# A chunk-wise first stage with columns and shifts on ScalarE, and two combinations of h made from negated halves and accumulating transfers

## Chip, cores and metric

One core of one Trainium2 chip runs the whole program as one launch. The metric is the device time in microseconds, the median of several runs. All arithmetic is fp32; each large product is made in three passes of fp32r matmuls, from a value's high part and its low part (the value less its high part): high x high, high x low, low x high.

## The reference, cut to what matters

A transformer of two layers with three sublayers each (feed-forward, mixer, feed-forward; the mixers are a pooling mixer and a latent attention), and two hybrid attention layers behind it. x is 512 tokens x 1024 features. The change touches the start of the program and the beginning of each of the four feed-forward stages:

```python
sc = jax.nn.silu(c)                                  # c: 1 x 1024
mod = (sc @ ada_w[i] + ada_b[i]).reshape(B, 9, D)    # ada_w[i]: 1024 x 9216
...
h = rmsnorm(x, g_pre) * (1.0 + scale) + shift        # shift, scale: rows 3k, 3k+1 of mod
gate, up = jnp.split(h @ w_in, 2, axis=-1)           # w_in: 1024 x 5632
y = (jax.nn.silu(gate) * up) @ w_out                 # w_out: 2816 x 1024
x = x + weight * (1.0 + gate_row) * rmsnorm(y, g_post)
```

## The kernel before

Everything lies transposed: features on the 128 partitions, tokens along the free dimension. x and h are eight chunks (c = 0 to 7) of 128 features x 512 tokens. Weights arrive in units of 128 x 1024 (512 KB) on SyncE's queue; ScalarE writes a unit's high part (`split_hi`, L444), VectorE its low part (`split_lo`, L459), TensorE multiplies (`three_passes`, L486). Four stages are feed-forward: ffn0, ffn1, ffn2, ffn3; between them lie pool and mla, and behind them two hybrid layers.

**The start.** X is loaded whole on ScalarE's queue; params, `ones` and `ident` on SyncE's. The 16 row blocks of ada_w for shift and scale (8 MB, `ada_first`) come in pairs on SyncE's and GpSimd's queues. VectorE multiplies them by silu(c) and adds them up (`first_rows_dve`, L840 to L860), TensorE closes both sums over partitions with one-column matmuls (`shift_pe` L836, `ada_close_pe` L896). ScalarE squares X chunk by chunk, TensorE sums each chunk's squares (L554), VectorE takes the reciprocal of the root and TensorE spreads it over partitions (`spread_pe`, L571). Only when all of shift and scale is there does `pre_dve`/`pre_act` make h: VectorE scales (L646), ScalarE writes h_hi (L632) and h_full (L635) with the shift as bias, VectorE writes h_lo (L655). TensorE then multiplies units 0 and 1 chunk by chunk and units 2 and 3 one after the other (`ffn_pe`, L1032).

**The beginning of a feed-forward stage.** Units 0 to 3 are plain. The other 20 column blocks of w_in go in ten "pairs" by Winograd's scheme of seven products per 2 x 2 block product (`pair_pe`, products 0 to 6, 24 matmuls of 256 columns each). For this four combinations of h's quarters are made once per stage: U, T2, T3, T4 (`combine_dve`, L1235). VectorE makes all four, each 128 x 1024: U = even chunks' first half of tokens less their second half; T2 = U + odd chunks' second half; T3 = odd second half less even second half; T4 = T2 less odd first half. ScalarE writes their high parts (`combine_hi_act`, L1128), VectorE their low parts over the sums themselves (`combine_lo_dve`, L1253; t_lo and t_sum share memory). Product 0 needs unit 4, product 1 unit 5 and U, product 2 unit 6 and T2, product 3 unit 7, product 4 unit 8 and T3, product 6 unit 10 and T4.

**What sets the order.** Each engine has its own instruction list, written out by hand, which runs in order; waits are on semaphores. GpSimd issues two kinds of transfers in order: the accumulating load that adds one weight unit to another (`add_weights`, L1306) and the loads of the later rows of ada_w (`ada_piece`, L1311), whose products VectorE takes between its other work (`ada_block_dve`, L885), two rows in each pair and the rest in the second half of the stage.

## Time and profile before

| | us |
|---|---|
| median of 3 runs (lowest, highest) | 2941.68 (2940.72, 2943.49) |
| the profiled execution | 2942.72 |
| its span | 2940.9 |
| TensorE busy in the span | 2807.1 (95%) |
| VectorE busy | 2184.5 (74%) |
| ScalarE busy | 1423.5 (48%) |
| GpSimd busy | 402.4 (14%) |

Times in rows are microseconds from the span's start, durations too unless ns stands there. PE is TensorE's matmul side, PEld its weight loads, DVE is VectorE, ACT ScalarE, POOL GpSimd, SP SyncE. One fp32 matmul makes two records. L444 is line 444 of the kernel.

### The profile page before, as it was taken

The page shows a single profiled execution, that of the slowest core. Times are in us where ns is not written, and L with a number is a line of the kernel's source. Part 1 is how long each engine was busy: PE and PEld are TensorE (multiplying, and loading weights), DVE is VectorE, ACT ScalarE, POOL GpSimd, SP SyncE. Part 2 cuts the span into 40 slices and gives each one's busy share as a digit, 9 for nine tenths or more (in the row PEclk, how much of TensorE's full clock was granted, in tenths as well). Part 3 has the DMA queues.
Part 4 walks back from the last instruction along what each step waited for, and adds up shares of the span by engine and source line. Part 5 has one row for each costly group of instructions (what it writes and reads, how often), then busy time and mean ns, then how long its engine had stood idle before and what let it go on. Part 6 is the DMA issues. An engine that isn't in the chain of part 4 may idle for free. (4 is left out here: it accounts for less than half of the span.)

```text
span 2940.9 us, 42829 instructions
## 1 busy us (share of the span) xinstructions
PE 2807.1 (95%) x16742; PEld 2452.6 (83%) x16742; DVE 2184.5 (74%) x3415; ACT 1423.5 (48%) x2356; POOL 402.4 (14%) x299
## 2 busy tenths in 40 slices
PE   7999989999999999889999999999899999999999
PEld 7998878998889988667789988887788778877887
DVE  6888678888788887789687755477777663876773
ACT  4455234455245552466455542463655434555552
POOL 1100102100100101100300000313300233141003
PEclk9999999999999999999999999999999999999999
DMA  6765641765636756200235533302211232022113
GB/s 247 214 207 173 225 154 34 222 210 168 220 123 201 225 161 215 81 18 19 100 101 159 151 101 100 129 22 77 95 51 56 95 122 79 28 95 72 51 58 115
DMA packets 100393, 365.82 MB, mean 124 GB/s; under 512 B 11616, under 2 KB 12384, under 8 KB 99552
## 3 DMA queue, kind: packets, MB, share of 16 engines
q1 hardware_dynamic: 72464, 257.25, 25.1%
q0 software_dynamic: 25280, 92.29, 11.5%
q10 hardware_dynamic: 2448, 13.54, 1.2%
q8 instruction: 134, 2.20, 0.3%
q14 instruction: 67, 0.55, 0.1%
HBM read 354.64 MB, written 6.29 MB: 123 GB/s over the span
## 5 line engine op out<-in xcount | busy, mean ns | idle before, releaser
L444 ACT ACTIVATE w_hi<-raw 128x1024 fp32r<-128x1024 f32 x353 | 368.0, 1052 | 299.1 <-DMA raw<-stream_in 188.2
L465 POOL TENSOR_TENSOR w_lo<-raw,w_hi 128x1024 fp32r<-128x1024 f32 x111 | 278.6, 2516 | 1296.4 <-ACT w_hi L444 1296.4
L486 PE MATMUL psum<-h_hi,w_hi 128*128 128x256 f32 (+1 forms) x1607 | 349.4, 329 | 15.0 <-DVE w_lo L459 9.6
L486 PE MATMUL psum<-h_hi,w_lo 128*128 128x256 f32 (+1 forms) x1607 | 343.1, 325 | 0.0
L486 PE MATMUL psum<-h_lo,w_hi 128*128 128x256 f32 (+1 forms) x1607 | 342.8, 325 | 0.0
L444 ACT ACTIVATE w_hi<-xr 128x1024 fp32r<-128x1024 f32 x200 | 211.3, 1057 | 264.7 <-DVE xr L1169 95.0
L459 DVE TENSOR_TENSOR w_lo<-raw,w_hi 128x1024 fp32r<-128x1024 f32 x202 | 247.2, 1227 | 87.6 <-ACT w_hi L444 87.5
L486 PE MATMUL psum<-t_hi,w_hi 128*128 128x256 f32 (+1 forms) x1536 | 284.5, 300 | 17.3 <-DVE a_lo L1091 8.8
L486 PEld LDWEIGHTS psum<-h_hi,w_hi 128*128 128x128 f32 x1607 | 251.7, 189 | 49.2 <-DVE w_lo L459 12.9
L486 PE MATMUL psum<-t_hi,w_lo 128*128 128x256 f32 (+1 forms) x1536 | 282.7, 299 | 0.0
L486 PEld LDWEIGHTS psum<-h_hi,w_lo 128*128 128x128 f32 x1607 | 252.7, 189 | 26.7
L486 PEld LDWEIGHTS psum<-h_lo,w_hi 128*128 128x128 f32 x1607 | 252.6, 189 | 26.9
L459 DVE TENSOR_TENSOR w_lo<-xr,w_hi 128x1024 fp32r<-128x1024 f32 x160 | 195.7, 1223 | 93.5 <-ACT w_hi L444 93.4
L486 PE MATMUL psum<-t_lo,w_hi 128*128 128x256 f32 (+1 forms) x1472 | 262.1, 294 | 0.0
L486 PEld LDWEIGHTS psum<-t_hi,w_hi 128*128 128x128 f32 x1536 | 220.2, 188 | 33.7 <-issue 11.9
L486 PEld LDWEIGHTS psum<-t_hi,w_lo 128*128 128x128 f32 x1536 | 221.6, 188 | 10.6
L486 PEld LDWEIGHTS psum<-t_lo,w_hi 128*128 128x128 f32 x1472 | 209.1, 188 | 8.0
L885 DVE SCALAR_TENSOR_TENSOR ada_raw<-ada_raw,silu_row 128x1024 f32<-128x1024 f32 x128 | 156.0, 1220 | 46.1 <-DMA ada_raw<-ada_in 45.9
L1311 POOL DMA_DIRECT2D ada_raw<-ada_in x126 | 67.0, 532 | 848.6 <-DVE ada_raw L885 844.4
L486 PE MATMUL psum<-a_lo,w_hi 128*128 128x512 f32 x704 | 177.1, 392 | 0.0
L486 PEld LDWEIGHTS psum<-a_lo,w_hi 128*128 128x128 f32 x704 | 132.6, 188 | 29.2
L1527 ACT ACTIVATE pt_hi<-psum 128x512 fp32r<-128x512 f32 (+3 forms) x160 | 74.6, 466 | 119.6 <-PE psum L1478 117.6
(510 smaller groups left out, 5550.8 us busy)
## 6 DMA issues: line engine op xcount, KB each, us to landing
raw<-stream_in SPq DMA_DIRECT2D x353, 512.0 KB, 3.4
ada_raw<-ada_in POOLq DMA_DIRECT2D x128, 512.0 KB, 5.4
xr<-stream_in SPq DMA_DIRECT2D x120, 512.0 KB, 4.6
xr<-stream_in POOLq DMA_DIRECT2D x40, 512.0 KB, 5.5
ada_first<-ada_in POOLq DMA_DIRECT2D x4, 1024.0 KB, 16.7
ada_first<-ada_in SPq DMA_DIRECT2D x4, 1024.0 KB, 22.1
x_held<-X ACTq DMA_DIRECT2D x2, 2048.0 KB, 6.8
X<-x_held ACTq DMA_DIRECT2D x2, 2048.0 KB, 8.3
```

The costliest lines, as they stand in the source:

```text
L444: act.activation(w_hi[:, u % RING], tile, ACT.Copy, scale=-1.0 if u in negated else 1.0).then_inc(hi_ready, 1)
L459: op = dve.tensor_tensor(w_lo[:, u % RING], source[u][0], low, ALU.subtract)
L465: pool.tensor_tensor(w_lo[:, u % RING], source[u][0], w_hi[:, u % RING].bitcast(F32), ALU.subtract).then_inc(lo_ready, 1)
L486: mm = pe.matmul(dst, w[wi], m[mi], start=(first and n == 0), stop=(last and n == total - 1), skip_group_check=skip)
L885: dve.scalar_tensor_tensor(out=row, in0=row, scalar=1.0, in1=silu_row[:], op0=ALU.mult, op1=ALU.mult, accum_out=mod[:, j, n:n + 1]).then_i ...
L1311: pool.dma_start(ada_raw[:, t % 2], ada[t]).then_inc(ada_loaded[t % 2], 16)
L1527: turned_hi.give(act.activation(A["place"](0, t, rows, n, i), psum[0:rows, 6 + k % 2, 0:n * P].rearrange("p (a n) -> p a n", n=P), ACT.Cop ...
```

## The change

Start: X comes in four pieces on SyncE's queue, with the blocks of ada_w behind it one by one, chunk c's scale block and then its shift block, and weight units 0 to 3 between them (2 and 3 go to the pair buffers); GpSimd loads nothing there. The first eight columns of params and `ident` come on ScalarE's queue. silu(c) is spread over a row by eight matmuls. The squares of X are summed by VectorE, then by TensorE once. scale is a dot product on VectorE for each chunk, shift one too for chunks 2, 4, 6, 7, and a matmul sum for chunks 0, 1, 3, 5. ScalarE makes the two columns of each chunk and then h_hi and h_full from h_full = X * rstd. TensorE multiplies units 0 and 1 with each chunk and units 2 and 3 with chunks that came earlier; filler matmuls (`keep_busy`) are added.

Each feed-forward stage: VectorE makes U and T2 alone. ScalarE writes the negated half of each chunk into T3 or T4 (8 activations of 128 x 256), and GpSimd issues two accumulating transfers, from h_full into T3 and from T2 into T4. In ffn1 and ffn2 two rows of ada_w move from the first pair to the second half of the stage.

```diff
...
+            if L == "ffn0":
+                plan_loads(u, u + 2)
+                for v, slot in ((u + 2, pair_slots[2]), (u + 3, pair_slots[0])):
+                    home[v] = (slot, None, cur.d)
+                    source[v] = (slot.tile, slot.sem, slot.plan())
+                    slot.free = (lo_ready, v + 1)
+                    cur.d += 1
...
+        def first_squares_act(act):
+
+            for c in range(NC):
+                if c % 2 == 0:
+                    act.wait_ge(x_loaded[c // 2], 16)
+                sq_ready.give(act.activation(square_tiles[c], X[:, c], ACT.Square, scale=1.0 / 32), ("ffn0", "pre", c))
+                if c == 3:
+                    act.wait_ge(row_spread, 1)
+                    act.activation(silu_row[:, 0:S], psum[:, 0], ACT.Copy)
+                    act.activation(silu_row[:, S:D], psum[:, 1], ACT.Copy).then_inc(row_ready, 1)
+            full_root_act(act, "ffn0")
...
+        def first_squares_dve(dve, order):
+
...
+            for c in range(1, NC):
+                dve.wait_ge(sq_ready.sem, sq_ready.at(("ffn0", "pre", c)))
+                op = dve.tensor_tensor(total, total, square_tiles[c], ALU.add)
+                if c < NC - 1:
+                    order.step(op)
+                else:
+                    x_squares.give(op, ("ffn0", "pre"))
...
         def full_pe(pe, L):
-            for c in range(NC):
-                pe.wait_ge(sq_ready.sem, sq_ready.at((L, "pre", c)))
-                sums.give(column_sums(pe, sq[:, c % 2], 4, 0, first=(c == 0)), (L, "pre", c))
+            pe.wait_ge(x_squares.sem, x_squares.at((L, "pre")))
+            sums.give(column_sums(pe, square_tiles[0], 4, 0, first=True), (L, "pre", NC - 1))
...
+                    if c:
+                        negate_act(act, L, c - 1)
                 if between is not None:
                     between(c)
+            if L in FFNS:
+                negate_act(act, L, NC - 1)
+
+        def negate_act(act, L, c):
+
+            x, part = ((T3, slice(HALF, S)), (T4, slice(0, HALF)))[c % 2]
+            act.wait_ge(full.sem, full.at((L, c)))
+            act.activation(t_sum[:, x, c // 2], h_full[:, c, part], ACT.Copy, scale=-1.0).then_inc(parts_negated, 1)
...
+        def row_pe(pe):
+
             pe.wait_ge(value.sem, value.at("silu_c"))
...
+                mm = pe.matmul(psum[:, k // 4, k % 4 * P:k % 4 * P + P], silu_c[:, k:k + 1].broadcast_to((P, P)),
+                               ident[:], start=(k % 4 == 0), stop=(k % 4 == 3), skip_group_check=True)
+            mm.then_inc(row_spread, 1)
+
+        def shift_pe(pe, c):
+
+            pe.wait_ge(first_loaded[c][0], 16)
+            for k in range(NC):
+                mm = pe.matmul(psum[:, 6, c:c + 1], first_block(c, 0)[:, k * P:k * P + P], silu_c[:, k:k + 1],
+                               start=(k == 0), stop=(k == NC - 1), skip_group_check=True)
+            mm.then_inc(shift_sums, 1)
...
+        def columns_act(act, c):
+
+            g = col.at["norm_g"] + c
+            act.wait_ge(mod_blocks, c + 1)
+            act.activation(acol[:, c:c + 1], mod[:, 1, c:c + 1], ACT.Identity, scale=par[:, g:g + 1],
+                           bias=par[:, g:g + 1]).then_inc(columns_made, 1)
+            made = c + 1 + sum(e < c for e in SHIFT_BY_PE)
+            if c in SHIFT_BY_PE:
+                b = col.at["ada_b"] + c
+                act.wait_ge(shift_sums, SHIFT_BY_PE.index(c) + 1)
+                act.activation(mod[:, 0, c:c + 1], psum[:, 6, c:c + 1], ACT.Identity,
+                               bias=par[:, b:b + 1]).then_inc(columns_made, 1)
+                made += 1
+            else:
+                act.wait_ge(shift_by_dve, c - sum(e < c for e in SHIFT_BY_PE) + 1)
+            act.wait_ge(columns_made, made)
...
+        def first_chunk_act(act, c):
+
+            act.wait_ge(scaled.sem, scaled.at(("ffn0", c)))
+            part_hi.give(act.activation(h_hi[:, c], h_full[:, c], ACT.Identity, scale=acol[:, c:c + 1],
+                                        bias=mod[:, 0, c:c + 1]), ("ffn0", c))
+            full.give(act.activation(h_full[:, c], h_full[:, c], ACT.Identity, scale=acol[:, c:c + 1],
+                                     bias=mod[:, 0, c:c + 1]), ("ffn0", c))
...
+        def dot_dve(dve, row, j, n):
+
+            b = col.at["ada_b"] + NC * j + n
+            return dve.tensor_tensor_reduce(out=row, in0=row, in1=silu_row[:], op0=ALU.mult, op1=ALU.add, scale=1.0,
+                                            scalar=par[:, b:b + 1], accum_out=mod[:, j, n:n + 1])
+
+        def first_dots_dve(dve, c):
+
+            dve.wait_ge(first_loaded[c][1], 16)
+            dot_dve(dve, first_block(c, 1), 1, c).then_inc(mod_blocks, 1)
+            if c not in SHIFT_BY_PE:
+                dve.wait_ge(first_loaded[c][0], 16)
+                dot_dve(dve, first_block(c, 0), 0, c).then_inc(shift_by_dve, 1)
...
+        def first_chunks_dve(dve, u0):
+
+            dve.wait_ge(spread.sem, spread.at(("ffn0", "pre")))
+            first_scale_dve(dve, 0)
+            split_lo(dve, u0)
+            split_lo(dve, u0 + 1)
+            first_low_dve(dve, 0)
+            for c in range(1, NC):
+                first_scale_dve(dve, c)
+                first_dots_dve(dve, c)
+                if c == 1:
+                    split_lo(dve, u0 + 2)
+                    continue
+                first_low_dve(dve, c - 1)
+                if c == 2:
+                    split_lo(dve, u0 + 3)
+            combine_u_dve(dve, "ffn0")
+            first_low_dve(dve, NC - 1)
...
-        FIRST_ROWS = {"ffn0": 2, "ffn1": 0, "ffn2": 0}
+        ROWS = {"ffn0": (16, 64), "ffn1": (64, 104), "ffn2": (104, 144), "ffn3": (144, 144)}
+        SHIFT_BY_PE = (0, 1, 3, 5)
+        FIRST_ROWS = {"ffn0": 2, "ffn1": 0, "ffn2": 0, "ffn3": 0}
+        PAIR_ROWS = {"ffn0": range(9), "ffn1": range(1, 9), "ffn2": range(1, 9), "ffn3": ()}
...
+        def first_chunks_pe(pe, L, u0, g0):
+
+            late = {2: (0, 1), 3: (2,), 4: (3,), 5: (4,), 6: (5,), 7: (6, 7)}
...
+            for c in range(NC):
+                if c in SHIFT_BY_PE[1:]:
+                    shift_pe(pe, c)
+                pe.wait_ge(h_ready.sem, h_ready.at((L, c)))
+                for m in range(2):
+                    chunk(m, c)
+                for m in range(2, 4):
+                    for late_c in late.get(c, ()):
+                        chunk(m, late_c)
+                if c < 2:
+                    keep_busy(pe, 7, 6)
...
+                row_pe(pe)
+                pe.wait_ge(small_loaded, 32)
+                keep_busy(pe, 7, 12)
                 full_pe(pe, L)
-                shift_pe(pe)
+                keep_busy(pe, 7, 4)
                 spread_pe(pe, (L, "pre"), 5, 5)
-                ada_close_pe(pe, 1, ada_acc)
-                dense_first(pe, L, u0, g0, 2)
-                dense(pe, u0 + 2, g0 + 2)
-                dense(pe, u0 + 3, g0 + 3)
+                shift_pe(pe, 0)
+                keep_busy(pe, 7, 8)
+                pe.wait_ge(row_ready, 1)
+                first_chunks_pe(pe, L, u0, g0)
...
-            act.wait_ge(combined.sem, combined.at((L, x)))
+            if x == T3:
+                act.wait_ge(odd_added, 16 * (FFNS.index(L) + 1))
+            elif x == T4:
+                act.wait_ge(t2_added, 16 * (FFNS.index(L) + 1))
+            else:
+                act.wait_ge(combined.sem, combined.at((L, x)))
             combined_hi.give(act.activation(t_hi[:, x], t_sum[:, x], ACT.Copy), (L, x))
...
-            pre_act(act, L, shift)
-            if L == "ffn0":
-                split_hi(act, u0 + 2)
-                split_hi(act, u0 + 3)
+                for c in range(NC):
+                    columns_act(act, c)
+                    first_chunk_act(act, c)
+                    if c >= 4:
+                        for e in {4: range(4)}.get(c, (c - 1,)):
+                            negate_act(act, L, e)
+                    if c < 2:
+                        split_hi(act, u0 + 2 + c)
+                negate_act(act, L, NC - 1)
             else:
+                pre_act(act, L, shift)
...
+        def combine_u_dve(dve, L):
+
+            even = h_full[:, 0:NC:2]
+            dve.wait_ge(full.sem, full.at((L, NC - 2)))
+            combined.give(dve.tensor_tensor(t_sum[:, U], even[:, :, 0:HALF], even[:, :, HALF:S], ALU.subtract), (L, U))
...
+            if L != "ffn0":
+                combine_u_dve(dve, L)
             dve.wait_ge(full.sem, full.at((L, NC - 1)))
-            combined.give(dve.tensor_tensor(t_sum[:, U], even[:, :, first], even[:, :, second], ALU.subtract), (L, U))
...
             combined.give(dve.tensor_tensor(t_sum[:, T2], t_sum[:, U], odd[:, :, second], ALU.add), (L, T2))
             combine_lo_dve(dve, L, U)
-            combined.give(dve.tensor_tensor(t_sum[:, T3], odd[:, :, second], even[:, :, second], ALU.subtract), (L, T3))
-            dve.wait_ge(combined.sem, combined.at((L, T2)))
-            combined.give(dve.tensor_tensor(t_sum[:, T4], t_sum[:, T2], odd[:, :, first], ALU.subtract), (L, T4))
...
             dve.wait_ge(combined_hi.sem, combined_hi.at((L, x)))
+            if x == T2:
+                dve.wait_ge(t2_added, 16 * (FFNS.index(L) + 1))
             combined_lo.give(dve.tensor_tensor(t_lo[:, x], t_sum[:, x], t_hi[:, x].bitcast(F32), ALU.subtract), (L, x))
...
+        def add_odd(pool, L):
+
+            pool.wait_ge(parts_negated, NC * (FFNS.index(L) + 1))
+            pool.wait_ge(full.sem, full.at((L, NC - 1)))
+            pool.dma_start(t_sum[:, T3], h_full[:, 1:NC:2, HALF:S], accum_op=ALU.add).then_inc(odd_added, 16)
+
+        def add_t2(pool, L):
+
+            pool.wait_ge(combined.sem, combined.at((L, T2)))
+            pool.dma_start(t_sum[:, T4], t_sum[:, T2], accum_op=ALU.add).then_inc(t2_added, 16)
...
-            add_weights(pool, L, 0)
-            t = ADA[L][0] * NC + 2 if ADA[L] else 18 * NC
-            if ADA[L]:
...
+            if L in ("ffn0", "ffn3"):
+                add_odd(pool, L)
+                add_weights(pool, L, 0)
+            else:
+                add_weights(pool, L, 0)
+                add_odd(pool, L)
+            add_t2(pool, L)
+            end = min(ROWS[L][1] + 2, 18 * NC)
+            pieces = iter(range(ROWS[L][0] + (0 if L == "ffn0" else 2), end))
+            for t in islice(pieces, FIRST_ROWS[L] + (2 if L == "ffn0" else 0)):
+                ada_piece(pool, t)
...
-            sp.dma_start(par[:], params).then_inc(small_loaded, 16)
-            sp.dma_start(ones[:], consts[:, ONES * P:(ONES + 1) * P]).then_inc(small_loaded, 16)
-            sp.dma_start(ident[:], consts[:, IDENT * P:(IDENT + 1) * P]).then_inc(small_loaded, 16)
-            for k in range(4, 8):
-                sp.dma_start(ada_first[:, 2 * k:2 * k + 2],
-                             ada[2 * k:2 * k + 2].rearrange("t p n -> p t n")).then_inc(first_loaded[k], 16)
-            sp.dma_start(silu_row[:], c_row).then_inc(row_loaded, 16)
+            for k in range(4):
+                sp.dma_start(X[:, 2 * k:2 * k + 2], xT[:, 2 * k:2 * k + 2]).then_inc(x_loaded[k], 16)
+                if k == 2:
+                    sp.dma_start(ones[:], consts[:, ONES * P:(ONES + 1) * P]).then_inc(small_loaded, 16)
+            sp.dma_start(par[:, NC:], params[:, NC:]).then_inc(small_loaded, 16)
+            for c in range(NC):
+                for which in (1, 0):
+                    sp.dma_start(first_block(c, which), ada[NC * which + c]).then_inc(first_loaded[c][which], 16)
+                if c < 2:
+                    for k in range(2):
+                        fetch(sp, own["ffn0", "u"] + 2 * c + k)
...
-            for k in (1, 2, 3, 0):
-                pool.dma_start(ada_first[:, 2 * k:2 * k + 2], ada[2 * k:2 * k + 2]
-                               .rearrange("t p n -> p t n")).then_inc(first_loaded[k], 16)
-            first = 2 * NC
-            for k in range(2):
-                pool.dma_start(ada_raw[:, k], ada[first + k]).then_inc(ada_loaded[k], 16)
-            for u in range(2):
-                low_gpsimd(pool, u)
...
-            act.dma_start(X[:], xT).then_inc(x_loaded, 16)
-            act.wait_ge(small_loaded, 48)
+            act.dma_start(par[:, 0:NC], params[:, 0:NC]).then_inc(c_loaded, 16)
+            act.dma_start(ident[:], consts[:, IDENT * P:(IDENT + 1) * P]).then_inc(c_loaded, 16)
+            act.wait_ge(c_loaded, 32)
             value.give(act.activation(silu_c[:], par[:, 0:8], ACT.Silu), "silu_c")
             act.wait_ge(evac.sem, 4)
-            act.wait_ge(x_loaded, 16)
-            full_act(act, "ffn0", [(X[:, c], None) for c in range(NC)])
+            first_squares_act(act)
             split_hi(act, 0)
             split_hi(act, 1)
-            act.wait_ge(row_loaded, 16)
-            act.activation(silu_row[:], silu_row[:], ACT.Silu).then_inc(row_ready, 1)
...
-            dve.wait_ge(small_loaded, 48)
-            dve.wait_ge(value.sem, value.at("silu_c"))
-            first_rows_dve(dve)
+            first_squares_dve(dve, order)
+            dve.wait_ge(small_loaded, 32)
+            dve.wait_ge(row_ready, 1)
+            first_dots_dve(dve, 0)
             full_dve(dve, "ffn0")
-            shift_dve(dve)
-            ada_close_dve(dve, 1)
-            dve.wait_ge(lo_ready, 2)
```

## Rows read from the trace of the kernel before

**Rows 1.** The page, part 1: busy time, share of the span, instructions.

```profile
PE 2807.1 (95%) x16742; PEld 2452.6 (83%) x16742; DVE 2184.5 (74%) x3415; ACT 1423.5 (48%) x2356; POOL 402.4 (14%) x299
```

**Rows 2.** Windows: PE, PEld, DVE, ACT, POOL busy; clock; DMA share; GB/s.

```profile
13.40:44.90 31.50, 29.41 (x136) 29.13 (x137) 18.34 (x22) 11.02 (x16) 4.66 (x2) 1.00 0.95 368
```

**Rows 3.** Timeline, the start: start, duration, engine, line, operation, out<-in, count.

```profile
13.40 13.88 PE L554 MATMUL psum<-ones,sq 128*128 128x64 f32 x64 [13.40 <-ACT sq L582]
34.13 3.58 PE L836 MATMUL psum<-ones,shift_acc 128*128 128x1 f32 x16
37.57 2.05 PE L571 MATMUL psum<-ident,stat 128*128 128x128 f32 x8
44.90 0.79 PE L510 MATMUL psum<-h_hi,w_hi 128*128 128x512 f32 x1 [2.08 <-ACT h_hi L632]
```

**Rows 4.** Timeline of PE, ffn0.

```profile
49.76 0.63 PE L486 MATMUL psum<-h_lo,w_hi 128*128 128x512 f32 x1
50.19 0.63 PE L486 MATMUL psum<-h_hi,w_hi 128*128 128x512 f32 x1
...
58.69 1.99 PE L486 MATMUL psum<-h_hi,w_hi 128*128 128x512 f32 x8
60.52 2.00 PE L486 MATMUL psum<-h_hi,w_lo 128*128 128x512 f32 x8
...
69.67 0.63 PE L486 MATMUL psum<-h_hi,w_hi 128*128 128x256 f32 x4
...
89.46 0.63 PE L486 MATMUL psum<-h_hi,w_hi 128*128 128x256 f32 x4
```

**Rows 5.** Timeline of DVE, ffn0: unit 4's low part, an ada_w row, unit 7's.

```profile
65.09 1.22 DVE L459 TENSOR_TENSOR w_lo<-raw,w_hi 128x1024 fp32r<-128x1024 f32 x1
...
73.10 1.22 DVE L885 SCALAR_TENSOR_TENSOR ada_raw<-ada_raw,silu_row 128x1024 f32<-128x1024 f32 x1
...
75.39 1.22 DVE L459 TENSOR_TENSOR w_lo<-raw,w_hi 128x1024 fp32r<-128x1024 f32 x1
```

**Rows 6.** Timeline, ffn0: an activation and a subtraction of one chunk.

```profile
49.97 0.71 ACT L635 ACTIVATE h_full<-tb,mod 128x512 f32<-128x512 f32 x1
50.67 0.75 DVE L655 SCALAR_TENSOR_TENSOR h_lo<-tb,mod,h_hi 128x512 fp32r<-128x512 f32 x1
```

**Rows 7.** DMA issues to 80 us: count, KB each, us to landing.

```profile
ident<-consts_in SPq DMA_DIRECT2D x1, 64.0 KB, 10.9
```

**Rows 8.** Timeline of PE around the end of pool.

```profile
463.51 1.07 PE L554 MATMUL psum<-ones,std 128*128 128x64 f32 x8
...
468.53 1.91 PE L554 MATMUL psum<-ones,ta 128*128 128x64 f32 x8
470.24 2.02 PE L571 MATMUL psum<-ident,stat 128*128 128x128 f32 x8
...
474.30 1.50 PE L565 MATMUL psum<-ones,ident 128*128 128x128 f32 x12
```

**Rows 9.** Timeline, the beginning of ffn1.

```profile
495.16 1.28 ACT L544 ACT_TABLE_LOAD   x1
...
498.79 1.22 DVE L1246 TENSOR_TENSOR t_sum<-h_full 128x1024 f32<-128x1024 f32 x1
...
501.06 1.22 DVE L459 TENSOR_TENSOR w_lo<-raw,w_hi 128x1024 fp32r<-128x1024 f32 x1
...
502.33 0.74 PE L486 MATMUL psum<-h_hi,w_hi 128*128 128x256 f32 x4 [2.89 <-DVE w_lo L459]
```

**Rows 10.** Timeline of PE, the beginnings of ffn2 and ffn3.

```profile
864.30 0.72 PE L486 MATMUL psum<-h_hi,w_hi 128*128 128x256 f32 x4 [2.88 <-DVE w_lo L459]
...
1499.70 1.23 PE L486 MATMUL psum<-h_hi,w_hi 128*128 128x256 f32 x4 [3.86 <-DVE w_lo L459]
...
1504.90 0.63 PE L486 MATMUL psum<-t_hi,w_hi 128*128 128x256 f32 x4
```

**Rows 11.** Line 1306, its 40 accumulating loads: landing.

```profile
DMA to landing us min/median/max: 5.2/5.5/7.6
```

More of the change, by code:

```diff
@@ L1 @@
 from contextlib import ExitStack
+from itertools import islice
 import numpy as np
@@ L122, in kernel_program @@
 def kernel_program(nc, stream, ada, xT, params, consts, constsr, pool_band, mla_rope, rope_cst,
-                   pos, w2, c_row, held, out, NU):
+                   pos, w2, held, out, NU):
     col = param_columns()
@@ L334, in plan_pre @@
             if L in FULL:
-                for c in range(NC) if L == "ffn0" else (NC - 2, NC - 1):
-                    (sq_ready if L == "ffn0" else x_squares).plan((L, "pre", c))
-                    sums.plan((L, "pre", c))
+                if L == "ffn0":
+                    sq_ready.plan(*[(L, "pre", c) for c in range(NC)])
+                    x_squares.plan((L, "pre"))
+                    sums.plan((L, "pre", NC - 1))
+                else:
+                    for c in (NC - 2, NC - 1):
+                        x_squares.plan((L, "pre", c))
+                        sums.plan((L, "pre", c))
                 for signal in (roots, inverses, spread):
@@ L365, in plan_ffn @@
             for x in (U, T2, T3, T4):
[L366 removed]
+                for signal in (combined,) * (x in (U, T2)) + (combined_hi, combined_lo):
                     signal.plan((L, x))
@@ new lines, in first_dots_dve, with first_scale_dve, first_low_dve @@
+        def first_dots_dve(dve, c):
[4 more added lines that the diff above has]
+                dot_dve(dve, first_block(c, 0), 0, c).then_inc(shift_by_dve, 1)
+        def first_scale_dve(dve, c):
+            scaled.give(dve.tensor_tensor(h_full[:, c], X[:, c], psum[:, 5], ALU.mult), ("ffn0", c))
+        def first_low_dve(dve, c):
+            dve.wait_ge(part_hi.sem, part_hi.at(("ffn0", c)))
+            dve.wait_ge(full.sem, full.at(("ffn0", c)))
+            h_ready.give(dve.tensor_tensor(h_lo[:, c], h_full[:, c], h_hi[:, c].bitcast(F32), ALU.subtract), ("ffn0", c))
@@ L1339, in ffn_sp @@
                 sp.wait_ge(prod.sem, prod.at(("u", u - 1)))
-            if L == "ffn0":
-                for k in range(NC):
-                    sp.wait_ge(first_loaded[k], 16)
             for name in ("a21", "a22", "last"):
                 fetch(sp, (L, 0, name))
-            if L != "ffn3":
+            if L not in ("ffn0", "ffn3"):
                 fetch(sp, u + 2)
@@ L3687 @@
         columns(doubled(a_(k_norm_g_2))), columns(cmp_b1_2), columns(cmp_pe_2)], 1)
-    first = a_(ada_w).reshape(2, NC, P, 9, D).transpose(0, 3, 1, 2, 4).reshape(144, P, D)[:2 * NC]
-    turned = a_(ada_w).transpose(0, 2, 1).reshape(144, P, D)[2 * NC:]
-    ada = np.concatenate([first, turned])
+    ada = np.array(a_(ada_w).transpose(0, 2, 1)).reshape(144, P, D)
+    for n in (0, 1, 3, 5):
+        ada[n] = a_(ada_w)[0, :, n * P:(n + 1) * P].reshape(NC, P, P).transpose(1, 0, 2).reshape(P, D)
     xT = a_(x)[0].T.reshape(NC, P, S).transpose(1, 0, 2)
```

167 lines of the change are left out of this document (52 added, 115 removed).

## The prediction

> **What bounds the kernel now.** I read the page's busy shares first, then the windows and the timeline of the start, then the timelines around the beginnings of the four feed-forward stages. TensorE is busy for 2807.1 of 2940.9 us [rows 1], so only its idle time, its filler and its half-pace time can be won. There are two such places here. One is the start: the first product begins at 44.90 [rows 3]. Before it, DMA is the limit (368 GB/s, a DMA share of 0.95) [rows 2]; behind it TensorE has no gap up to product 0 of pair 0 at 69.67, and pair 1 begins at 89.46, so a pair takes 19.8 and one of its seven products 2.83 [rows 4]. The other is a wait before product 0 in ffn1, ffn2 and ffn3, of 2.89, 2.88 and 3.86, each for unit 4's low part from VectorE [rows 9, 10]. In ffn3 a half-pace product follows: 1499.70 to 1504.90 is 5.20, against 2.83, so 2.4 more [rows 4, 10].
>
> **The start, part by part.** I set a schedule against the mark "pair 1 at 89.46".
>
> Loads: X, constants, 16 blocks and four units are about 12.9 MB. At 368 GB/s [rows 2] that is 35 us, so with some 2 us of first latency chunk 7's last block lands near 37. The path below needs it at about 58, so DMA leaves the path.
>
> Chunk 0: `ident` landed 10.9 after its issue as third on a shared queue [rows 7]. It now has its own queue behind eight columns; I bound its landing by 5 and 11 and take 7. The eight row matmuls are 16 records at 2.05/8 [rows 3], 4.1 us: 11.3. ScalarE's two copies and its last four squares (six that take 0.71 each at most, as the row of this size [rows 6]) are some 4 us, and VectorE's last addition ends near 16. The sums of squares are 8 of the 64 records that took 13.88 [rows 3], 1.7, or half that at full pace; root and reciprocal 0.5; the spread 2.05 or half: about 20.5. The shift of chunk 0 by TensorE is 16 one-column records: 3.58 [rows 3] at half pace, about 1.8 at full; I take 2.5. Then ScalarE adds the bias (0.2, an estimate), writes two results of 0.71, and VectorE subtracts, 0.75 [rows 6]: 2.4, or 2.6 with the handovers. Chunk 0 starts at about 25.5, 19.4 us earlier than now.
>
> TensorE from there: 96 matmuls (four units, eight chunks, three passes) at (60.52 - 58.69)/8 = 0.229 [rows 4] are 22.0. Two fillers of 12 records are 1.5 each, 3.0. Now the part that costs: the shift matmuls of chunks 1, 3 and 5 stand in TensorE's queue behind the whole work of the chunk before. After each of them come ScalarE's and VectorE's steps, and TensorE waits for h_ready. That is 1.8 + 2.6 = 4.4 us without useful work, three times: 13.2. VectorE doesn't set this: a dot product costs about 1.22, as the row products do [rows 5] (the new instruction has no row; below 0.75 or above 2.5 I don't expect it), its whole list over the eight chunks is some 30 us, which from 21 on ends near 51, before the three round trips do. Sum: 25.5 + 22.0 + 3.0 + 13.2 = 63.7 at full pace throughout.
>
> The clock: early matmuls of 512 columns ran 0.43 apart (49.76 to 50.19), which is the lower of the two levels, 1.2 GHz, and 0.229 apart later, the upper, 2.4 GHz [rows 4], although PE had been busy for 29.41 of 31.50 [rows 2], with 64-column sums and one-column closings. At the end of pool the same sums ran with full pace and then lost it (8 records in 1.07, then 1.91) [rows 8]. A round trip is 4.4 us of one-column matmuls and idling, more than the wait of 3.86 that cost 2.4 in ffn3 [rows 10]. Three such falls would be 7.2, none 0. I take 4.0, as some will meet the clock at its old level: product 0 at 67.7. The Trainium skill, TensorE: Matmul & The Clock Gate, Part 1, says that the gate follows how busy the array has been and that a sustained busy stretch brings the full rate; read plainly, fillers and shifts count as busy and the sum stays at 63.7. The trace disagrees as far as thin matmuls go (29.41 busy of 31.50, and half pace behind it).
>
> Pair 0: VectorE now needs 65.09 to 76.61, 11.5 us, from the beginning of unit 4's low part to the end of unit 7's [rows 5]. Product 3 is due 3 x 2.83 = 8.5 after product 0. Unit 4's low part will begin about 1 us before product 0 (chunk 7 is followed by 18 matmuls, 4.1 us, on TensorE and by three VectorE steps, 3.4, ahead of it). So product 3 waits 11.5 - 1 - 8.5 = 2.0. Pair 1: 67.7 + 19.8 + 2.0 = 89.5. That is the old time: 19 us won at chunk 0 are all given back, and the start is worth 0, with ends of -6 (full pace, no wait) and +6 (`ident` at 11 and all falls of the clock).
>
> **The combinations, part by part.** In ffn1 two VectorE steps (T3, T4) go from ahead of unit 4's low part: 501.06 - 498.79 = 2.27 [rows 9]. ScalarE gets eight negations of 256 columns, about 0.4 each by half of 0.71 [rows 6]. Six lie in its idle time between chunks; the last two stand before the table load (1.28 at 495.16 [rows 9]) and so before U's high part, and with the hops take back 0.5. Product 0 comes 1.8 earlier in ffn1, and so in ffn2. In ffn3 the wait falls from 3.86 to about 1.6, and the half-pace product (2.4) should go with it: after a wait of 2.89 the first four matmuls took 0.74, after 3.86 they took 1.23 [rows 9, 10]. That would be 4.7.
>
> The new waits: ScalarE waits for both transfers ahead of unit 7's high part, and VectorE waits for the transfer out of T2 before it overwrites T2. Queued behind that are T2's low part, a gate product and unit 6's low part, 1.14 + 0.60 + 1.14, about 2.9, for which product 2 waits. In ffn1 T2 is made at about 497.6 and product 2 is due at 502.33 - 1.8 + 2 x 2.83 = 506.2. So a transfer may take 506.2 - 2.9 - 497.6 = 5.7 from issue to landing. The nearest row is the accumulating load of 512 KB from HBM: 5.2, median 5.5, 7.6 at most [rows 11]. From SBUF to SBUF, in 1 KB pieces for T3 and two in flight, there is no row; I bound it by 4 and 10 and take 5.5, the median. Then there is almost nothing to wait for; I leave 0.7 of ffn3's 4.7 for the tighter order there: 4.0. The Trainium skill, DMA: Bandwidth & Descriptors, Anatomy of one DMA, has 2.0 us and the bytes at 436 GB/s, which gives 3.2 as an estimate; the row's 5.5 is longer, and the sum would not change, as the transfer is hidden either way. Two rows of ada_w less in pair 0 of ffn1 and ffn2 I cost at nothing: VectorE has room there once product 0 runs, and the second half of the stage takes them in 2 of 24 units of over 4 us each. GpSimd's loads of ada_w rows stand behind the new transfers, but need VectorE's rows anyway.
>
> Sum: 0 - 1.8 - 1.8 - 4.0 = -7.6. The profiled execution took 2942.72, so 2935.1; the median of the runs lies 1.0 below it, so 2934.1.
>
> **The rivals.** (A) The clock holds through the round trips and the start gains: 4.0 of half pace go, and a little of product 3's wait. For it: at the end of pool 128-column matmuls (470.24, 8 records in 2.02) were followed by a rise (474.30, 12 in 1.50) [rows 8], and the fillers are of that kind. Against it: no row shows one-column matmuls that hold full pace; those of the start ran at half [rows 3]. The start gives -5: 2929. (B) The start is late instead: `ident` near 11 as before [rows 7] and every fall of the clock paid, +6 there: 2940. (C) The other side: the transfers are slow. Every us beyond 5.7 delays product 2 in ffn1, ffn2 and ffn3 by one, and in ffn0 once the 2.0 before product 3 are used up. The gain of 7.6 is gone when 3x + (x - 2) = 7.6, x = 2.4, a transfer of 8.1. At 10 it is 3 x 4.3 + 2.3 = 15.2 given back: +7.6, or 2949. For it: two in flight and small pieces; against it: the median of 40 accumulating loads beside the weight stream is 5.5 [rows 11].
>
> **How the numbers follow.** Forecast 0.42, A 0.25, B 0.18, C 0.15. About 0.2% (5.9 us) is what a measurement of this kernel can tell from no change. The forecast lies 7.6 below with 4 to either side from the clock and the landing, so two thirds of it count as faster; A counts as faster, B as the same, most of C as slower. Faster 0.57, same 0.30, slower 0.13. The range reaches from beyond A to C's point of balance: 2925 to 2944.
>
> **What would show it.** First chunk product near 25 and product 0 of pair 0 in ffn0 near 68. Three gaps of TensorE of about 2.6, each behind 16 one-column records. A wait near 2 before product 3 in ffn0, pair 1 near 89.5. Waits before product 0 of about 1 in ffn1 and ffn2 and 1.6 in ffn3, and 0.7, not 1.2, for its first four matmuls. Landings of the new transfers near 5.5. The forecast is wrong if pair 1 of ffn0 is off 89.5 by over 4, or if product 2 waits more than 1 us in the later stages.

## The result, and the profile after

The changed kernel's median is 2952.75 us (six runs, 2946.17 to 2959.62), against 2941.74 for the kernel before (six runs, 2937.14 to 2947.16). The ratio is 1.004, with a 95% interval of 1.0027 to 1.0053: 11 us slower, where I forecast 7.6 faster. The profiled execution took 2959.36, at the upper end of its runs, with a span of 2957.6 (before: 2940.9).

The page after, part 1, against [rows 1]: TensorE's busy time grew by 12.5 of the 16.7 us of span, with only 32 more records, so most of the loss is time in which TensorE works slowly.

```profile
PE 2819.6 (95%) x16774; PEld 2461.4 (83%) x16774; DVE 2181.3 (74%) x3423; ACT 1438.3 (49%) x2401; POOL 404.4 (14%) x301
```

The timeline of TensorE in ffn0 after the change (start, duration, engine, line, operation, operands, count, idle time before and its releaser), against [rows 3, 4]:

```profile
23.00 0.47 PE L506 MATMUL psum<-h_hi,w_hi 128*128 128x512 f32 x1 [1.16 <-issue]
...
25.79 1.84 PE L875 MATMUL psum<-silu_c,ada_in_t 128*128 128x1 f32 x16
30.34 0.79 PE L506 MATMUL psum<-h_hi,w_hi 128*128 128x512 f32 x1 [2.70 <-DVE h_lo L926]
...
43.89 0.79 PE L506 MATMUL psum<-h_hi,w_hi 128*128 128x512 f32 x1 [2.70 <-DVE h_lo L926]
...
56.14 0.79 PE L506 MATMUL psum<-h_hi,w_hi 128*128 128x512 f32 x1 [2.70 <-DVE h_lo L926]
...
68.60 0.63 PE L506 MATMUL psum<-h_hi,w_hi 128*128 128x256 f32 x4
...
76.51 0.71 PE L506 MATMUL psum<-t_hi,w_hi 128*128 128x256 f32 x4 [2.09 <-DVE w_lo L476]
...
82.60 1.06 PE L506 MATMUL psum<-h_lo,w_hi 128*128 128x256 f32 x4
...
86.01 0.63 PE L506 MATMUL psum<-t_hi,w_hi 128*128 128x256 f32 x4
...
94.49 0.63 PE L506 MATMUL psum<-h_hi,w_hi 128*128 128x256 f32 x4
```

The first chunk starts at 23.00, and three gaps of 2.70 stand before chunks 1, 3 and 5, the first behind 1.84 of one-column matmuls; each is followed by half pace. Product 0 of pair 0 comes at 68.60, 1.1 earlier than before. Then product 2 waits 2.09 and product 3 2.01, part of product 3 runs at half pace (four 256-column matmuls in 1.06, not 0.63), and pair 1 comes at 94.49: 5.0 later than before.

Windows of the changed kernel from the first chunk to product 0, and from there to pair 1 (columns as in [rows 2]): a mean granted clock of 0.78 and 0.93 says how much of this stands at the lower level.

```profile
23.00:68.60 45.60, 37.50 (x168) 31.68 (x169) 29.96 (x43) 21.27 (x39) 4.31 (x5) 0.78 0.53 179
68.60:94.49 25.89, 21.79 (x170) 21.41 (x169) 21.40 (x24) 11.67 (x15) 2.49 (x5) 0.93 0.77 247
```

What product 2 waited for, in VectorE's timeline of ffn0 and then of ffn3, and TensorE's beginning of ffn3, against [rows 5, 10]:

```profile
73.40 1.22 DVE L1347 TENSOR_TENSOR t_lo<-t_sum,t_hi 128x1024 fp32r<-128x1024 f32 x1 [2.15 <-DMA t_sum<-t_sum]
74.55 0.68 DVE L1354 TENSOR_TENSOR a<-ta,psum 128x512 f32<-128x512 f32 x1
75.14 1.22 DVE L476 SCALAR_TENSOR_TENSOR w_lo<-xr,w_hi 128x1024 fp32r<-128x1024 f32 x1
...
1505.03 0.74 PE L506 MATMUL psum<-h_hi,w_hi 128*128 128x256 f32 x4 [1.57 <-DVE w_lo L479]
...
1511.98 1.22 DVE L1347 TENSOR_TENSOR t_lo<-t_sum,t_hi 128x1024 fp32r<-128x1024 f32 x1 [4.06 <-DMA t_sum<-t_sum]
...
1515.08 0.71 PE L506 MATMUL psum<-t_hi,w_hi 128*128 128x256 f32 x4 [4.13 <-DVE w_lo L476]
```

T2's low part overwrites what the transfer reads, so it waits; a gate product and unit 6's low part stand behind it on VectorE, and product 2 needs the last. ffn3 began as forecast (a wait of 1.57, 0.74 for the first four matmuls) and lost it two products later.

The beginning of ffn1 after, against [rows 9]; the same two waits stand in ffn2, with 1.20 and 0.87:

```profile
504.91 0.74 PE L506 MATMUL psum<-h_hi,w_hi 128*128 128x256 f32 x4 [1.20 <-DVE w_lo L479]
...
511.70 0.74 PE L506 MATMUL psum<-t_hi,w_hi 128*128 128x256 f32 x4 [0.87 <-ACT std L1147]
```

The landings (issue to landing, KB each) of T2's transfer into T4, in ffn0, in ffn1 and in ffn3:

```profile
t_sum<-t_sum POOLq DMA_DIRECT2D x1, 512.0 KB, 9.3
...
t_sum<-t_sum POOLq DMA_DIRECT2D x1, 512.0 KB, 6.1
...
t_sum<-t_sum POOLq DMA_DIRECT2D x1, 512.0 KB, 8.9
```

T3's transfer took 6.3, 5.5, 5.5 and 5.7 in the four stages. Laying the matmuls of both traces side by side, the changed kernel is behind by 5.0 at pair 1 of ffn0, 4.3 at the end of pool, 3.8 behind the first products of ffn1, 2.1 at 600, 9.0 behind the first products of ffn3, and 16.6 at the end. So 7.6 of the 16.7 arose behind 1530, in code that the change doesn't touch, at places where one trace has a half-pace stretch and the other a shorter one or none; 3.9 more arose so at 830 to 845. The medians, 11 apart, are the measure; this one pair of profiles exaggerates.

### The profile page after: what moved, and what is told of

The parts are those of the page before. It is cut to its first block and busy times, and to the rows that moved or that the text cites. A ratio compares the mean times of both kernels' runs of the same rounds, so it can differ in the third digit from the quotient of the medians.

```text
span 2957.6 us, 42977 instructions
## 1 busy us (share of the span) xinstructions
PE 2819.6 (95%) x16774; PEld 2461.4 (83%) x16774; DVE 2181.3 (74%) x3423; ACT 1438.3 (49%) x2401; POOL 404.4 (14%) x301
```

## The experiments

All ran in three sets, each with the kernel before on the same chip; the medians of the kernel before in the sets were 2940.95, 2944.19 and 2940.54. The changed kernel stands in none of these sets, so what is said against it goes by the two ratios to the kernel before, and such a difference is known to some 5 us either way (an estimate from the two intervals). A ratio is worked out over the single runs and is not quite the quotient of the medians (for e5 that would be 0.9965). "Product 0" and "pair 1" are the times in ffn0 in each trace (before: 69.67 and 89.46; the changed kernel: 68.60 and 94.49, ratio 1.0040).

| run | median us | ratio to before | 95% interval | product 0 | pair 1 |
|---|---|---|---|---|---|
| e1 start only | 2946.91 | 1.0019 | 1.0010 to 1.0028 | 70.43 | 93.17 |
| e2 combinations only | 2946.24 | 1.0018 | 1.0010 to 1.0027 | 69.97 | 92.68 |
| e3 T4 on VectorE | 2940.64 | 0.9999 | 0.9989 to 1.0009 | 67.66 | 90.83 |
| e4 shift early | 2940.72 | 0.9993 | 0.9985 to 1.0002 | 55.97 | 83.21 |
| e5 early, T4 on VectorE | 2933.91 | 0.9956 | 0.9940 to 0.9972 | 59.26 | 82.02 |
| e6 early, no transfer | 2937.60 | 0.9977 | 0.9968 to 0.9987 | 60.25 | 82.98 |
| e7 weights last | 2945.72 | 1.0007 | 0.9998 to 1.0016 | 68.42 | 93.85 |
| e8 20 fillers | 2956.15 | 1.0035 | 1.0023 to 1.0046 | 66.51 | 93.04 |
| e9 early, weights last | 2934.23 | 0.9979 | 0.9967 to 0.9991 | 56.05 | 82.07 |
| e10 10 fillers | 2947.45 | 1.0028 | 1.0016 to 1.0041 | 66.92 | 95.02 |
| e11 e5, rows moved | 2936.01 | 0.9981 | 0.9969 to 0.9993 | 59.40 | 79.84 |
| e12 T3 only | 2941.56 | 1.0008 | 0.9997 to 1.0019 | 68.47 | 90.27 |

**e1, the start alone.** The changed kernel without the combinations:

```diff
-            if L in ("ffn0", "ffn3"):
-                add_odd(pool, L)
...
-            add_t2(pool, L)
+            add_weights(pool, L, 0)
...
+            combined.give(dve.tensor_tensor(t_sum[:, T3], odd[:, :, second], even[:, :, second], ALU.subtract), (L, T3))
```

> The chunk-wise start alone: T3 and T4 are made by VectorE again, no negation by ScalarE, no accumulating transfer from h_full or t_sum. Theory (the trace of the changed kernel puts pair 1 of ffn0 5.0 us later than before, of which 2.1 are product 2 waiting behind a transfer and the rest the start): the start costs about 3 in ffn0, product 2 of pair 0 does not wait for a low part behind a transfer, product 0 stays near 68.6, and the half-pace stretches behind the three gaps stay; 2947 us against about 2942 for the kernel before, 6 under the changed kernel. Rival (the start is worth nothing, all of the loss is the transfers): 2942, equal to before. Rival 2 (the transfers gain, the start loses it all): 2955 or more.

The start alone costs 6.0, as the theory had it (e1 keeps the moved rows of ada_w). Pair 1 is 3.7 late: the three gaps are there, 2.70 each, with a half-pace stretch of 3.4 behind each, and product 3 waits 1.46. In this trace the first chunk came 2.3 later than in the changed kernel's, though TensorE's instructions up to it are the same. Its timeline there:

```profile
21.90 3.76 PE L585 MATMUL psum<-ones,ident 128*128 128x128 f32 x16
25.31 0.77 PE L506 MATMUL psum<-h_hi,w_hi 128*128 128x512 f32 x1
```

A half-pace stretch of 10.2 began at 16.7, the fillers took 3.76, and the first chunk came at 25.31, not 23.00. Of the eleven traces with this start, five have it so (e1, e5, e6, e10, e11: 25.3 to 25.5) and six have 22.8 to 23.4. No edit goes with it, so up to 2.5 us in the columns "product 0" and "pair 1" are chance.

**e2, the combinations alone**, in the kernel before (its start kept; the same negations, `add_odd` and `add_t2`).

> The two combinations by negations and transfers alone, with the start of the kernel before. Theory: ffn0's product 2 has 4 us of slack there and does not wait; ffn1 and ffn2 gain 1.7 at product 0 and give 1.0 to 1.5 back before product 2, because ScalarE's queue stands at T4's high part until the transfer lands; in ffn3 product 0 comes at full pace 2 to 3 earlier and product 2 waits 4; sum within 1 of before: 2942. Rival (the transfers are the loss of the joined change): 2950. Rival 2 (as I forecast, they gain): 2935.

5.3 slower: about halfway between my theory (no change) and the rival with the loss. The two parts, 6.0 and 5.3, make up the 11.0 of the joined change. Timelines of e2, ScalarE and TensorE in ffn0, then TensorE in ffn3:

```profile
65.40 1.06 ACT L445 ACTIVATE w_hi<-raw 128x1024 fp32r<-128x1024 f32 x1 [3.23 <-DMA raw<-stream_in]
...
80.25 0.74 PE L487 MATMUL psum<-h_hi,w_hi 128*128 128x256 f32 x4 [1.96 <-DVE w_lo L460]
...
1507.09 1.19 PE L487 MATMUL psum<-t_hi,w_hi 128*128 128x256 f32 x4 [3.88 <-DVE w_lo L457]
```

ScalarE began unit 4's high part at 65.40 (before: 60.88), as the load of the weights was late, and VectorE's queue moved back with it: ffn0, where I had counted slack, lost 3.2. In ffn3 the wait of 3.88 is long enough for half pace behind it (four matmuls in 1.19).

**e3, T4 back on VectorE, T3 still by transfer.**

```diff
-            x, part = ((T3, slice(HALF, S)), (T4, slice(0, HALF)))[c % 2]
+            if c % 2:
+                return
+            x, part = T3, slice(HALF, S)
...
-            if x == T2:
-                dve.wait_ge(t2_added, 16 * (FFNS.index(L) + 1))
...
+            combined.give(dve.tensor_tensor(t_sum[:, T4], t_sum[:, T2], odd[:, :, first], ALU.subtract), (L, T4))
```

> The changed kernel with T4 made by VectorE as before (one more 1.14 us instruction in each ffn stage), T3 still by negation and transfer; no transfer out of t_sum, so T2's low part waits for none. Theory: the waits before product 2 of pair 0 go (2.1 in ffn0, 0.9 in ffn1 and ffn2, 4.1 in ffn3), and product 0 of ffn1 to ffn3 comes 1.1 later; 0.2 to 2.1 gained in ffn0, 0 in ffn1 and ffn2, 3.0 in ffn3: 5 under the changed kernel, 2948. Rival (the landing of T3's transfer takes over as what product 2 waits for): no change, 2953. Rival 2: VectorE's place is dearer than the wait, 2955.

0.9999 against 1.0040: 12 under the changed kernel, where I expected 5. Product 2 no longer waits for a low part behind a transfer in any stage: it waits 0.36 in ffn0, for ScalarE.

```profile
73.84 0.74 PE L506 MATMUL psum<-t_hi,w_hi 128*128 128x256 f32 x4 [0.36 <-ACT std L1149]
```

The wait before product 0 grew, as one step came back: to 2.04 in ffn1 and 2.72 in ffn3. Laid beside the changed kernel's trace, the stage beginnings give 5.6 us (3.6 in ffn0, 2.0 in ffn3, nothing over ffn1 and ffn2 together); no wait shows the rest of the 12. Against e1, in the same set, e3 is 6 faster, which is T3's transfer with this start.

**e4, the shift matmuls one place earlier.**

```diff
-                if c in SHIFT_BY_PE[1:]:
-                    shift_pe(pe, c)
+                if c and c + 1 in SHIFT_BY_PE:
+                    shift_pe(pe, c + 1)
...
+                if c == 0:
+                    shift_pe(pe, 1)
```

> The changed kernel with TensorE's shift matmuls of chunks 1, 3 and 5 one place earlier in its queue: chunk 1's before the fillers behind chunk 0, chunk 3's before the products of chunk 2, chunk 5's before those of chunk 4. Theory: the round trip (2.7 us three times) is what opens the gaps before chunks 1, 3 and 5, and the half pace follows them; chunk 1 comes 1 to 1.5 earlier, the gaps before chunks 3 and 5 go and at least two of the three half-pace stretches with them; product 0 of pair 0 at 58 to 61 in place of 68.6, 7 to 10 gained at pair 1, 2944. Rival (VectorE's dots and ScalarE's chunks are the next bound, right behind the gaps): gaps of 1.5 to 2 stay, the half pace too, and 2 to 3 are gained, 2950. Rival 2 (pair 0 then waits for its weights' low parts as much longer): product 0 earlier, pair 1 unmoved, 2953.

As the theory had it, and stronger. Timeline of TensorE and the window from the first chunk to product 0:

```profile
29.32 0.50 PE L506 MATMUL psum<-h_hi,w_hi 128*128 128x512 f32 x1 [1.75 <-DVE h_lo L926]
...
48.98 0.50 PE L506 MATMUL psum<-h_hi,w_hi 128*128 128x512 f32 x1 [0.58 <-DVE h_lo L926]
...
65.71 1.19 PE L506 MATMUL psum<-t_hi,w_hi 128*128 128x256 f32 x4 [4.13 <-DVE w_lo L476]
```

```profile
22.82:55.97 33.15, 30.82 (x168) 26.09 (x169) 29.70 (x43) 21.29 (x39) 4.31 (x5) 1.00 0.67 237
```

The gaps are 1.75 and 0.58 and the third is gone, the granted clock is 1.00, and the stretch takes 33.15 in place of 45.60: 12.4, of which 5.8 is gap time ((3 x 2.70) - 1.75 - 0.58) and the rest, 6.7, the pace of the products. Then product 2 waits 4.13 for the transfer that product 0 has outrun.

**e5 and e6: both causes taken away.** e5 has e3's and e4's edits, e6 has e4's with no transfer at all.

> The changed kernel with both earlier edits: the shift matmuls of chunks 1, 3 and 5 one place earlier, and T4 made by VectorE (T3 by negation and transfer). Each alone was 12 under the changed kernel. Theory (the two causes lie one behind the other in ffn0, and with an early product 0 the landing of the second transfer had taken 4.1 of the 13.7 gained; without it pair 1 comes 9 to 10 before that of the kernel before, in place of 6.3; ffn3 gains 3 to 4 more): 2931. Rival (they overlap, what one frees the other had freed): 2937. Rival 2 (VectorE, with T4 back and an early pair 0, is late with the low parts of the weights): 2940.

> The changed kernel's start with the shift matmuls one place earlier, and no negation and no transfer at all: T3 and T4 by VectorE as before. Theory (T3's transfer is worth 6 with the late shifts, 2940.6 against 2946.9, and as much here): 2937. Rival (with an early product 0, landing of T3's transfer, 5.5 to 6.3, is as late as VectorE would be, and the two come out alike): 2931 to 2933. It also shows the start alone without its gaps: 4 faster than the kernel before by the theory, against 6 slower with them.

e5 is the fastest of the study and beats both kernels: 0.44% under the kernel before (0.28 to 0.60%). e6 is 0.23% under it, so the start without its gaps, with the moved rows of ada_w that e6 keeps, is a gain, and T3's transfer is worth something on top, though the intervals of the two touch. e11 below has e5's edits and one more, and came out at 0.9981: some 0.2 to 0.4% is what e5 can be said to gain.

**e7, the load of weights behind both transfers.**

```diff
                 add_odd(pool, L)
+                add_t2(pool, L)
                 add_weights(pool, L, 0)
```

> The changed kernel with GpSimd's three accumulating transfers of ffn0 and ffn3 in the order h_full, t_sum, weights, in place of h_full, weights, t_sum; ffn1 and ffn2 are as they were. Theory (the transfer out of t_sum takes 9.3 and 8.9 in ffn0 and ffn3 against 6.1 in ffn1 and ffn2 because the accumulating load of weights is in flight with it): its landing falls to 6 to 7, the waits before product 2 fall from 2.1 and 4.1 to 0 and 2, the weights come 1 later and are not waited for; 2949. Rival (the landing is long whatever the order, as the weights' load still overlaps it): 8.5 to 9, 2953. Rival 2 (the load of weights becomes the late one): product 1 or 3 waits and it is 2955.

The landings of T2's transfer in e7, in ffn0 and in ffn3:

```profile
t_sum<-t_sum POOLq DMA_DIRECT2D x1, 512.0 KB, 7.0
...
t_sum<-t_sum POOLq DMA_DIRECT2D x1, 512.0 KB, 6.3
```

From 9.3 and 8.9: its place behind two other accumulating transfers is what made it long. Now the load of weights is last, and takes 9.1 and 8.2 in place of 7.2 and 7.3. The Trainium skill, DMA: Bandwidth & Descriptors, Issuing engines are not separate DMA queues, says that all transfers interleave on the same engines, whoever starts them. These three all come from GpSimd; across two issuing engines e12 below agrees (3.6 becomes 6.6).

Product 2 waits 1.40 and 1.54. In ffn0 the 0.7 won there was nearly all lost again at product 3 (2.61 for 2.01), in part as one of GpSimd's loads of ada_w, behind all three transfers, came 0.41 late for VectorE:

```profile
78.57 1.23 DVE L952 SCALAR_TENSOR_TENSOR ada_raw<-ada_raw,silu_row 128x1024 f32<-128x1024 f32 x1 [0.41 <-DMA ada_raw<-ada_in]
...
81.00 1.23 PE L506 MATMUL psum<-h_hi,w_hi 128*128 128x256 f32 x4 [2.61 <-DVE w_lo L479]
```

The ratio falls from 1.0040 to 1.0007, 10 us, of which the traces show 0.6 in ffn0 and 3.1 in ffn3.

**e8 and e10, fillers in the gaps.** The edit is one line behind `shift_pe(pe, c)`: `keep_busy(pe, 7, 20)`, and 10 in e10.

> The changed kernel with 20 filler matmuls (about 2.3 us at full pace) behind the shift matmuls of chunks 1, 3 and 5, inside the gaps of 2.7, so that the gaps stay as long but TensorE is not idle in them. It parts the two costs of a gap: the time itself and the half pace behind it. Theory (the three half-pace stretches of 6.8 cost some 7 to 8 of chunks' products): the granted clock stays full from chunk 1 to chunk 7, product 0 of pair 0 at 61 to 63 in place of 68.6, of which 3 are given back before products 2 and 3; 2947. Rival (the half pace comes from the start's low use of TensorE at large, not from the gaps): stretches stay, 2953. Rival 2 (the fillers end after the low part of the chunk and delay it): 2956.

> The changed kernel with 10 fillers (20 records, 2.35 us) behind the shift matmuls of chunks 1, 3 and 5: the run with 20 had them 4.71 long, 2.0 longer than the gap, so its gaps were 2 longer each. Theory (half pace costs 7 to 8 of the chunks' products): no half-pace stretch between chunk 1 and 7, product 0 of pair 0 at 60 to 61, and then product 2 waits 3 to 4 for its low part behind the second transfer; ratio 1.0015 to 1.002 against 1.0040 of the changed kernel. Rival (the gain is all given back before pair 1): 1.0035 as with 20. Rival 2 (stretches of half pace stay): product 0 at 68.

e8 was mis-sized. A filler is two records, so 20 took 4.71 and ended 1.9 behind the chunk's low part. Row and window of e8:

```profile
27.44 4.71 PE L585 MATMUL psum<-ones,ident 128*128 128x128 f32 x40
...
22.93:66.51 43.58, 43.58 (x288) 39.57 (x289) 29.96 (x43) 21.27 (x39) 4.31 (x5) 1.00 0.53 183
```

All the same it parts the costs: chunks 1, 3 and 5 each start 1.63 later behind their shift than in the changed kernel (6.18 for 4.55; 4.9 in all), and yet the stretch is 2.0 shorter than the changed kernel's 45.60, at a granted clock of 1.00, so the half pace had cost 6.9, as in e4 (6.7). Then product 2 waits 3.21, with half pace behind it, and pair 1 is as late as in e1. e10's product 0 did not come at 60 to 61: a half-pace stretch lay at 16.8 to 27.0, before the first gap, and chunk 1 came 3.2 later than in the changed kernel; T2's transfer then took 10.5, and product 2 waited 5.11. It doesn't repeat e8's cleaner reading, and neither pays at the end.

**e9, both transfers, early shift, weights last** (the edits of e4 and e7).

> The changed kernel with the earlier shift matmuls and GpSimd's order h_full, t_sum, weights in ffn0 and ffn3: both transfers kept. Theory (the second transfer is dear where it lands late, and the order takes its landing to 6.3 to 7): product 2 of pair 0 waits 1 to 2 in ffn0 in place of 4.1, and 1.5 in ffn3; ratio to the kernel before 0.997. Rival (with product 0 early the landing is as long as the weights' transfer was late, no gain over the earlier shifts alone): 0.9993. Rival 2 (it equals the kernel with T4 on VectorE, 0.9956): the second transfer costs nothing once its landing is short.

Near the theory: product 2 waits 1.94 in ffn0 and 1.58 in ffn3, and it is 0.2% under the kernel before. Product 3 of ffn0 waits 2.66, in part for a late row of ada_w, as in e7. So both parts of the change can stay as they are, given the two orders.

**e11, two ada_w rows out of VectorE's way before product 3** (`FIRST_ROWS` of ffn0 0, two rows more in the down stage).

> The fastest so far (shift matmuls one place earlier, T4 by VectorE) with the two ada_w rows that VectorE reads ahead of pair 0's product 3 in ffn0 moved to the down stage (rows 1 and 2 of its list one higher). Theory (product 3 waits 1.46 for its low part, which stands behind these two rows, 2.3 us, in VectorE's queue): the wait goes, nothing is late in the down stage, 1.5 gained, ratio 0.995. Rival (VectorE is as late at the next step, ScalarE's square before product 4 or the rows in the down stage): no change, 0.9956.

Product 3 no longer waits and pair 1 comes at 79.84, 2.2 earlier than in e5. In this trace it was lost again between 240 and 300, where a half-pace stretch of 6.8 at 276 follows; the median is no better than e5's. Nothing is gained at the end.

**e12, T3 alone, in the kernel before.**

> The kernel before with T3 alone by ScalarE's negations and one accumulating transfer; T4 stays on VectorE; the start is that of the kernel before. Theory (one 1.14 us instruction less on VectorE ahead of product 0 in ffn1 to ffn3, landings of 5.5 that nothing waits for): 0.9 gained in ffn1 and ffn2, 1.2 to 3 in ffn3; ratio 0.9985. Rival (in ffn0 the transfer lies beside the load of weight unit 4, which came 3.2 late in the run with both combinations alone, so ffn0 loses 3): 1.000. Rival 2 (the loss of the combinations alone, 1.0018, is the first transfer's): 1.0018.

1.0008, nearest to its first rival. Product 0 waits 2.06, 2.04 and 2.72 in the later stages in place of 2.89, 2.88 and 3.86, but ffn0 lost 0.8 by pair 1 (product 3 waits 1.04 for its low part). The loads of weights issued from 52 to 75, in the kernel before and then in e12, by issuer, count, KB each and landing:

```profile
raw<-stream_in SPq DMA_DIRECT2D x3, 512.0 KB, 3.6
...
raw<-stream_in SPq DMA_DIRECT2D x3, 512.0 KB, 6.6
```

T3's transfer beside them takes their landing from 3.6 to 6.6: this is rival 1's mechanism. By the ratios alone e2 (1.0018) and e12 (1.0008) can't be parted; by the traces e2 has in addition the waits of product 2.

## Why the prediction was wrong, step by step

**Where the miss lies.** The forecast was -7.6 and the medians say +11.0, 18.6 apart. By the medians the start cost 6.0 for 0 (e1) and the combinations 5.3 for -7.6 (e2). In the two profiles the stage beginnings come to +5.0 in ffn0 for 0, -0.3 in ffn1 and again in ffn2 for -1.8 each, and +1.3 in ffn3 for -4.0: 5.7 for -7.6. The other 5 of the 11.0 no wait at a stage beginning shows.

**Chunk 0 and the round trips: right.** 23.00 for 25.5, three gaps of 2.70 for 2.6, DMA no limit. Product 0 at 68.60 for 67.7.

**The half pace: too small.** I took 4.0 of a bound of 7.2; e4 has 6.7 and e8 6.9. Chunk 0's lead of 2.5 paid for most of the difference, which is why product 0 looks right. That was luck: in five of the eleven traces with this start the lead is not there (e1). The half pace is rival B's second half. The Trainium skill, TensorE: Matmul & The Clock Gate, HAM oscillation, describes it for waits on a DMA: a wait that recurs each round throws the array back to the low clock each time. Here the wait is for two other engines, and the traces agree: 0.78 with the gaps, and 1.00 with e4's or with e8's fillers.

**What a wait's length says of the clock: too much read into it.** I read from two rows that a wait of 2.89 keeps the full pace and 3.86 loses it. In the fourteen traces all three waits of 3.84 to 3.87 before product 0 are followed by half pace, but so are 6 of 18 waits of 2.0 to 2.9: in ffn3 the first four matmuls take 0.74 after 2.71 (e5) and 1.22 after 2.72 (e12).

**Product 3's wait: the number right (2.01 for 2.0), in part by luck.** Without the wait for the transfer it is 1.46 and 1.47 (e1, e3). In the changed kernel a second wait stands in front of it, and half pace that cost 1.6 in product 3 behind it. Product 2 was to have room in ffn0 and waited 2.09. With these the start and ffn0 are worth +5.0, not 0.

**The failing step: "the new waits", a transfer of 5.5 that hides.** Its form was right: product 2 waits for what the transfer takes beyond about 6, with the queue I named behind it. The size was wrong where it matters. I took the median of loads that start at least 18 us apart; T2's transfer is the last of three that GpSimd starts within 2.4 and 3.0 us in ffn0 and ffn3, and the second of two in ffn1 and ffn2, and took 9.3, 6.1, 6.1 and 8.9. By my own rule ffn3's 8.9 costs 3.2; product 2 waited 4.13, and with the half pace behind it 5.9 were lost. That is rival C, to which I gave 0.15, and whose point of balance, 8.1, two stages passed and two did not. e3 takes the cause away (no wait of product 2 for it), e7 shortens the landing by the order alone. The range's upper end, 2944, was called C's point of balance; that is 2941.7.

**A queue that I named and did not cost.** ScalarE waits for the same transfer before T4's high part, and behind it stand two high parts and the snapshot of product 1. In ffn1 and ffn2 this is what product 2 waits for (0.87, released by ScalarE), though the landing was only 6.1. The squares before product 4 came 0.2 to 0.4 later as well. Of the 1.7 won at product 0 in ffn1 1.4 were given back, and again in ffn2. In ffn3 -4.0 became +1.3.

**Two ada_w rows "at nothing": they gained.** Between 509 and 600 the changed kernel made up 1.5, e3 2.4 and e1, whose only edit in that stretch is these rows, 1.9; e2 and e12, which keep the rows in pair 0, made up 0.0 and 0.6.

**ffn0's cover for the combinations was not there.** e2 has unit 4's high part 4.5 later and pair 1 3.2 late; e12 has the landings of 6.6 for 3.6. I had costed the transfers' share of the DMA engines at zero because none of my rows showed contention.

**The profiles' later 7.6 is not explained by the change.** The time at half pace (2 x span x (1 - mean granted clock)) was 92 us on average over the 33 runs of the kernel before in the first set and 118 over the changed kernel's six, of which the stretches behind the three gaps are 20; e4 has 101 and e9 93. Within the runs of most kernels a us of it goes with 0.2 to 0.5 us of time. Why single stretches later fall in one run and not in another stays open.

## What to carry to other kernels

A matmul whose result comes back to TensorE through two other engines belongs one stage of work ahead in TensorE's queue: here each gap cost its length, 2.7, and another 2.2 to 2.3 at half pace behind it. An accumulating transfer in place of a VectorE step is free only if everything queued behind its readers has that time too, on each engine that waits for it. Where several are started together, the one that is waited for goes first, and its landing is to be taken from a row with as many in flight.

## What the hardware showed that I had not expected

In e2 the 256-column matmuls of ffn3 ran faster than in the kernel before, both at a granted clock of 1.00 with TensorE never idle. The window 1545 to 1680 of the kernel before, then of e2:

```profile
1545.00:1680.00 135.00, 135.00 (x1148) 135.00 (x1148) 102.09 (x103) 72.47 (x89) 5.95 (x7) 1.00 0.53 160
...
1545.00:1680.00 135.00, 135.00 (x1194) 135.00 (x1193) 106.25 (x108) 75.39 (x93) 5.91 (x7) 1.00 0.55 165
```

1194 in place of 1148 in the same time: 113 against 118 ns each, which took 6.7 us off that stage, from pair 1 to its end, in that run. Shorter stretches of it stand in other traces, also in the changed kernel's ffn1. No edit goes with it and I have no cause; it adds to the scatter of some 3 to 5 us between runs of one kernel.

An accumulating transfer of 512 KB from SBUF to SBUF landed in 5.4 to 6.5 when first, 6.1 as second of two, 6.3 to 7.1 as second of three and 8.3 to 10.5 as last of three; the first is no faster than the accumulating loads from HBM [rows 11].
